# A pooled mixer computed in the other order, a three-product inverse, and a weight split placed later

## The chip, the cores and the metric

One core of one Trainium2 chip runs the whole program in one launch. The metric is the device time of the launch in microseconds, here the median of three runs of the kernel before: 2472.41 us (2469.35 to 2473.65).

## What is computed

A stack of three blocks on x of 512 tokens by 1024 features, all in f32. Block one is a gated delta rule mixer with 8 heads and a gated feed-forward. Then comes a modulated norm, a **pooled mixer** and a feed-forward with a short convolution, then differential attention and another such feed-forward, and a last norm. The parts that matter here:

```python
def modulate(h, shift, scale): return h * (1.0 + scale) + shift
# end of block one, which is the input of the pooled mixer's residual
x = modulate(rms_norm(x, normf_w), shf, scf)
# the delta rule, per head and chunk
t_inv = triangular_solve(eye + lower, eye, lower=True, unit_diagonal=True)
# pooled mixer on rms_norm(x, mix_norm)
for g, win in enumerate((2, 4, 8, 16)):       # 256 features each
    mean = (cs[hi] - cs[lo]) / (hi - lo)      # moving mean over tokens, window win, cut at the ends
    parts.append(mean - x_g)
y = einsum('bsgc,gce->bsge', pooled, w) * scale
```

## The kernel before

**Layout.** Activations lie feature-major: `x[:, m]` is 128 features by 512 tokens, eight such tiles. A product of f32 accuracy is made of three of rounded operands (`fp32r`): `term` (L1854 on) issues w_hi by h_hi, w_hi by h_lo and w_lo by h_hi, each with 512 moving columns. Every 128-column block of every weight is a "tile": SP loads it into `raw` (two slots), ScalarE copies it to `w_hi`, VectorE writes `w_lo = raw - w_hi` (L1111), and TensorE uses it. Both `split`s run four tiles ahead of TensorE and wait in their engine's queue for the slot that the product of four tiles before used. So weights stream in program order, and each engine's program places its own splits by hand among its other work.

**The heads.** `head` (L2005 for TensorE, L1334 for VectorE, L837 for ScalarE, L586 for POOL) computes one head of the delta rule while TensorE fills its waits with the next head's weight tiles. The tables HEAD_FILL and LAST_FILL say how many eighths of a tile (three products) stand ahead of each step. The inverse is built in six levels by doubling blocks. With X the inverse so far and U its transpose, a level does: `y` = masked lower part by X (bank 4), VectorE adds the identity into y_t; `u` = y_t by u_t (bank 6), ScalarE copies it to u_t; TensorE turns u_t (`x` step, bank 5), and VectorE copies that to x_t for the next level. VectorE and ScalarE also do the next head's short convolutions (`conv_taps`, `conv_silu`, `conv_tap`) and splits between these steps; the first split after the fifth level on ScalarE and the `short_conv` on VectorE need weight tile 4 of the head to be finished.

**A norm.** `norm` (L1949) sums squares over features by TensorE with one-column products (`sums`), VectorE writes mean plus eps (L1133), POOL takes the power -1/2 (L560), TensorE spreads it over rows (bank 3), and VectorE multiplies x by it. POOL adds up the first seven squares while a projection runs, ScalarE makes the last. Ahead of the mean VectorE has the last weight split of the projection behind it.

**The pooled mixer.** After the first feed-forward's down projection (DOWN[0], L1608) a norm writes the new x (`normed`), with squares for a second norm. That norm's factor is spread, and VectorE builds for each group of two feature tiles the sums over 2, 4, 8 and 16 tokens by doubling (`double`, L444; POOL does the widest), corrects the ends with `edges`, subtracts the centre (L1662), ScalarE and VectorE split the result into p_hi and p_lo, TensorE multiplies it with W in 48 wide products, and VectorE adds it to x (L1682).

**SP** loads in the order of its program. Four small loads for the attention stand behind the three ATT_Q tiles, with a wait until the down projection before is finished, and ahead of the next tiles' loads:

```python
sp.wait_ge(tile_done, ATT_Q.tile0)
for n, name in enumerate(("diff_lam_q1_2", "diff_lam_k1_2", "diff_lam_q2_2", "diff_lam_k2_2")):
    sp.dma_start(lam_in[0:1, n, :], a[name]).then_inc(lam_in_s, 16)
```

## Time and profile before

| | |
|---|---|
| median of 3 runs | 2472.41 us |
| the profiled execution, its own time | 2468.45 us |
| its span | 2466.8 us |
| TensorE busy | 2238.9 us (91%) |
| VectorE busy | 1315.5 us (53%) |
| ScalarE busy | 873.1 us (35%) |
| POOL busy | 652.0 us (26%) |
| chain that ended last | PE 72%, DVE 13%, issue 7%, ACT 4%, DMA 1%, POOL 1% |

Busy time is the time in which an engine has an instruction under way; a matmul's end is modelled, so the distance of two starts tells more than one's length. The chain is followed back from the last instruction to what released it. DVE is VectorE, ACT ScalarE, PE TensorE, SP the engine that issues loads.

### The profile page before, as it was taken

What the parts mean: (1) busy time and instruction counts of PE and PEld (TensorE: products, weight loads), DVE (VectorE), ACT (ScalarE), POOL (GpSimd) and SP (SyncE); (2) the same over time, 40 slices, a digit from 0 to 9 for tenths busy, and PEclk for the clock granted to TensorE, in tenths of its full rate; (3) what the DMA queues carried; (4) which work ended last, traced back from release to release, by engine and by line L of the source; (5) the groups of instructions that cost most, each with busy time, mean ns of one, the idle gap of its engine ahead of it and who ended that gap; (6) DMA issues with size and microseconds to landing.
All of it is one profiled execution on the core that took longest, in us unless ns stands there. A gap on an engine that the chain in (4) does not pass through costs nothing.

```text
span 2466.8 us, 31197 instructions
## 1 busy us (share of the span) xinstructions
PE 2238.9 (91%) x10502; PEld 1800.6 (73%) x10502; DVE 1315.5 (53%) x1755; ACT 873.1 (35%) x1287; POOL 652.0 (26%) x645
## 2 busy tenths in 40 slices
PE   5799999999889989999984999998888886999998
PEld 5677777777778868888873888887666564888887
DVE  6667655665643444334337544432676766444432
ACT  1322322232212223232223544421565654444421
POOL 3378666776660030000112000011032322000011
PEclk6999999999989999999996999999899997999999
DMA  6333333332323322333330233333111110333332
GB/s 213 84 100 93 85 86 101 95 87 84 95 69 95 99 79 85 97 98 90 98 94 17 85 94 95 96 94 95 46 43 60 43 60 26 94 94 101 91 94 73
DMA packets 351925, 211.44 MB, mean 86 GB/s; under 512 B 8649, under 2 KB 339843, under 8 KB 351876
## 3 DMA queue, kind: packets, MB, share of 16 engines
q1 hardware_dynamic: 343130, 184.67, 25.8%
q0 software_dynamic: 7680, 25.17, 3.4%
q10 hardware_dynamic: 1065, 0.96, 0.1%
q8 instruction: 29, 0.48, 0.1%
q14 instruction: 21, 0.16, 0.0%
HBM read 208.67 MB, written 2.10 MB: 85 GB/s over the span
## 4 chain that ended last, share of the span: by engine, by line
PE 72%; DVE 13%; issue 7%; ACT 4%; DMA 1%; POOL 1%; ACTq 0%; DVEq 0%; POOLq 0%; SPq 0%
PE ps L1858 21%; PE ps L1860 20%; PE ps L1859 20%; PE ps L2027 4%; PE ps L1896 3%; ACT at_swap L1020 2%; DVE w_lo L1111 1%; DVE small L1768 1%; ACT w_hi L697 1%; DVE gd_y_t L1422 1%; DVE gd_x_t L1445 1%; PE ps L1976 1%; DMA ada<-w_ada 1%; DVE gd_q_g L1410 1%; DVE at_rot L1746 0%
## 5 line engine op out<-in xcount | busy, mean ns | idle before, releaser
L1858 PE MATMUL ps<-h_hi,w_hi 128*128 128x512 f32 x1896 | 778.2, 410 | 28.3 <-DVE h_lo L1178 7.0
L1111 DVE TENSOR_TENSOR w_lo<-raw,w_hi 128x1024 fp32r<-128x1024 f32 x335 | 449.9, 1344 | 601.8 <-ACT w_hi L697 601.0
L1860 PE MATMUL ps<-h_hi,w_lo 128*128 128x512 f32 x1896 | 751.7, 396 | 0.0
L1859 PE MATMUL ps<-h_lo,w_hi 128*128 128x512 f32 x1896 | 750.1, 396 | 0.0
L697 ACT ACTIVATE w_hi<-raw 128x1024 fp32r<-128x1024 f32 x335 | 354.0, 1058 | 726.4 <-PE ps L1860 675.0
L1858 PEld LDWEIGHTS ps<-h_hi,w_hi 128*128 128x128 f32 x1896 | 364.1, 192 | 98.3 <-issue 25.2
L1860 PEld LDWEIGHTS ps<-h_hi,w_lo 128*128 128x128 f32 x1896 | 362.5, 191 | 79.1
L1859 PEld LDWEIGHTS ps<-h_lo,w_hi 128*128 128x128 f32 x1896 | 364.2, 192 | 65.6
L547 POOL TENSOR_TENSOR sq_sum<-x 128x512 f32<-128x512 f32 x5 | 5.2, 1040 | 947.5 <-DVE x L1620 522.3
L1858 PE MATMUL ps<-act_hi,w_hi 128*128 128x512 f32 x528 | 205.4, 389 | 0.0
L1859 PE MATMUL ps<-act_lo,w_hi 128*128 128x512 f32 x528 | 205.4, 389 | 0.0
L1860 PE MATMUL ps<-act_hi,w_lo 128*128 128x512 f32 x528 | 205.4, 389 | 0.0
L591 POOL TENSOR_TENSOR ada_w<-ada_w 128x256 f32<-128x256 f32 x144 | 132.3, 918 | 11.3
L1858 PEld LDWEIGHTS ps<-act_hi,w_hi 128*128 128x128 f32 x528 | 99.1, 188 | 20.6
L1860 PEld LDWEIGHTS ps<-act_hi,w_lo 128*128 128x128 f32 x528 | 99.1, 188 | 20.6
L1859 PEld LDWEIGHTS ps<-act_lo,w_hi 128*128 128x128 f32 x528 | 99.1, 188 | 20.6
L591 POOL TENSOR_TENSOR ada_w<-ada_w,cact 128x512 f32<-128x512 f32 x96 | 109.9, 1144 | 2.9 <-DMA ada_w<-w_ada 2.0
L674 POOL TENSOR_TENSOR x<-x,wo_s 128x512 f32<-128x512 f32 x56 | 74.2, 1342 | 112.8 <-ACT wo_s L1045 112.8
L551 POOL TENSOR_TENSOR sq_tmp<-x 128x512 f32<-128x512 f32 x31 | 34.9, 1127 | 226.3 <-DVE x L1620 144.8
L976 ACT ACTIVATE act_hi<-tmp 128x512 f32 x66 | 41.7, 632 | 131.4 <-DVE tmp L1602 87.7
L1605 DVE TENSOR_TENSOR act_lo<-tmp,act_hi 128x512 f32 x66 | 45.7, 693 | 61.1 <-ACT act_hi L976 61.1
L875 ACT ACTIVATE gd_u_t<-ps 128x512 f32<-128x512 f32 x48 | 28.6, 595 | 131.6 <-PE ps L2027 131.6
(314 smaller groups left out, 2850.1 us busy)
## 6 DMA issues: line engine op xcount, KB each, us to landing
raw<-ffn_w_up SPq DMA_DIRECT2D x88, 512.0 KB, 3.8
raw<-w_in SPq DMA_DIRECT2D x72, 512.0 KB, 3.8
raw<-w_ffn_in SPq DMA_DIRECT2D x44, 512.0 KB, 3.8
ada_w<-w_ada POOLq DMA_DIRECT2D x64, 256.0 KB, 3.3
raw<-ffn_w_down SPq DMA_DIRECT2D x32, 512.0 KB, 3.6
raw<-diff_w_qkv SPq DMA_DIRECT2D x24, 512.0 KB, 3.7
ada<-w_ada SPq DMA_DIRECT2D x4, 2048.0 KB, 15.3
ada_w<-w_ada_f POOLq DMA_DIRECT2D x32, 256.0 KB, 3.2
```

Of the source, the lines that this page charges most:

```text
L591: nc.gpsimd.tensor_tensor(dst, a, b, op).then_inc(ada_own, 1)
L674: nc.gpsimd.tensor_tensor(x[:, m], x[:, m], wo_s[:, m % 4], ADD).then_inc(wo_add, 1)
L697: nc.scalar.activation(w_hi[:, tile.slot], raw[:, tile.raw], ACT.Copy).then_inc(hi_ready, 1)
L976: nc.scalar.activation(dyn(act_hi, 2 * i + j), tmp[:, 4 + j], ACT.Copy).then_inc(f_hi, 1)
L1020: swapped = nc.scalar.activation(at["swap"][32 * q:32 * q + 32], ps[32 * (q ^ 1):32 * (q ^ 1) + 32, b, :], ACT.Copy)
L1111: nc.vector.tensor_tensor(w_lo[:, tile.slot], raw[:, tile.raw], w_hi[:, tile.slot].bitcast(F32), SUB)\
L1605: nc.vector.tensor_tensor(dyn(act_lo, 2 * i + j), gu, dyn(act_hi, 2 * i + j).bitcast(F32), SUB)\
L1858: nc.tensor.matmul(dst, w_hi[:, tile.slot, k], hi, start=first, stop=False)
L1859: nc.tensor.matmul(dst, w_hi[:, tile.slot, k], lo, start=False, stop=False)
L1860: return nc.tensor.matmul(dst, w_lo[:, tile.slot, k], hi, start=False, stop=last)
L1896: return nc.tensor.transpose(dst, src, ident[0:n_rows, 0:n_rows])
L2027: ins = nc.tensor.matmul(part(bank(b), n), part(lhs, n), part(rhs, n), start=True, stop=True)
```

## The change

Three parts.

**The inverse.** x_{n+1} is no longer u_t turned but a product of its own from the old u_t and y_t, issued ahead of the u products. The fills are quarters of a tile (six products) now, with no fill between x and u except at the last level, and none ahead of the w products.

```diff
-HEAD_FILL = dict(kv_tokens=2, g_rows=2, kk_qk=2, kb_rows=4, x_pairs=6, y0=1, w=1, o_sums=4, o_norm_rows=4)
...
+HEAD_FILL = {name: 1 for name in PE_STEPS if name != "w" and name not in [f"u{_n}" for _n in range(LEVELS - 1)]}
+HEAD_FILL.update(kb_rows=2, x_pairs=3, o_sums=2, o_norm_rows=2)
+LAST_FILL = {name: 1 for name in ["kv_tokens", "g_rows", "kk_qk", "kb_rows"] + [f"y{_n}" for _n in range(LEVELS)]}
+LAST_FILL.update(x_pairs=2, o_sums=2, o_norm_rows=2)
...
                     by_chunk(4, low_part[n % 2], x_t).then_inc(g_pe, 1)
+                    fill(f"x{n}")
+                    after_dve(f"y{n}")
+                    if n:
+                        after_act(f"u{n - 1}")
+                    if n < LEVELS - 1:
+                        by_chunk(5, u_t, y_t).then_inc(g_pe, 1)
                     fill(f"u{n}")
-
-                    after_dve(f"y{n}")
                     by_chunk(6, y_t, u_t).then_inc(g_pe, 1)
-                    if n < LEVELS - 1:
-                        fill(f"x{n}")
-                        after_act(f"u{n}")
-                        by_chunk(5, u_t, None, True).then_inc(g_pe, 1)
```

TensorE, head loop, before: from the u products of the third level (gd_u_t, gd_y_t) to the fill behind the turn of u_t (cst, gd_u_t). Products with h and w are fills.

```order
L2027 MATMUL ps<-gd_u_t,gd_y_t 128x128 [waits g_dve]
L2027 MATMUL ps<-gd_u_t,gd_y_t 128x128 x3
L1858 MATMUL ps<-h_hi,w_hi 128x512
L1859 MATMUL ps<-h_lo,w_hi 128x512
L1860 MATMUL ps<-h_hi,w_lo 128x512
L2020 REGISTER_ALU
L1896 MATMUL ps<-cst,gd_u_t 128x128 [waits g_act]
L1896 MATMUL ps<-cst,gd_u_t 128x128 x3
L1858 MATMUL ps<-h_hi,w_hi 128x512
```

The same place after the change: from the wait for y_t.

```order
L2016 REGISTER_ALU
L2019 REGISTER_ALU [waits g_dve]
L2026 MATMUL ps<-gd_y_t,gd_u_t 128x128 [waits g_act]
L2026 MATMUL ps<-gd_y_t,gd_u_t 128x128 x3
L2026 MATMUL ps<-gd_u_t,gd_y_t 128x128 x4
L1866 MATMUL ps<-h_hi,w_hi 128x512
L1867 MATMUL ps<-h_lo,w_hi 128x512
L1868 MATMUL ps<-h_hi,w_lo 128x512
```

The turn and the fill ahead of it are gone; eight products of x and u stand together (x first), and the fill behind them is twice as long.

**The late split.** `token_factor` takes the last tile of the stage before and splits it after the mean is written; the loops of the projections are written out so that their last output leaves this split out. In the same move the four small attention loads go to `masks`, which is free by then, ahead of the second feed-forward's tiles, and SP's wait is gone.

```diff
-            def token_factor(r):
+            def token_factor(r, late=None):
                 if r != N_MIX:
                     mean_squares(r)
+                if late is not None:
+
+                    split(late)
+
                 dve.wait_ge(n_pe, 2 * r + 2)
...
+            sp.wait_ge(tile_done, DOWN[0].tile(9, 1).before + 1)
+            sp.dma_start(bands[:], a["const_bands"]).then_inc(bands_in, 16)
             sp.dma_start(pos_i[0:1, :], a["positions_2"].rearrange("(o t) -> o t", o=1)).then_inc(pos_in, 16)
+            for n, name in enumerate(("diff_lam_q1_2", "diff_lam_k1_2", "diff_lam_q2_2", "diff_lam_k2_2")):
+                sp.dma_start(lam_in[:, n // 2, n % 2], a[name]).then_inc(lam_in_s, 16)
```

VectorE at the attention's norm, before: the last update of x, the split, the loop's end, the mean (small<-ps), the first use of the factor.

```order
L1620 TENSOR_TENSOR x<-x,ps 128x512
L1110 REGISTER_ALU
L1111 TENSOR_TENSOR w_lo<-raw,w_hi 128x1024 [waits hi_ready]
L1629 REGISTER_ALU
L1629 COMPARE_AND_BRANCH
L1133 TENSOR_SCALAR small<-ps 128x4 [waits n_pe]
L1187 SCALAR_TENSOR_TENSOR tmp<-x,vec,ps 128x512 [waits n_pe]
```

After the change:

```order
L1630 TENSOR_TENSOR x<-x,ps 128x512 [waits tile_done]
L1140 TENSOR_SCALAR small<-ps 128x4 [waits n_pe]
L1118 TENSOR_TENSOR w_lo<-raw,w_hi 128x1024 [waits hi_ready]
L1186 SCALAR_TENSOR_TENSOR tmp<-x,vec,ps 128x512 [waits n_pe]
```

The split now stands behind the mean, and the loop's branch is gone.

**The mixer.** W is applied first, on x as the down projection leaves it. With G = (1 + scale) * normf_w * mix_norm per feature, `weighted` makes h_hi and h_lo = split of x * G inside the down projection's loop, and sums over features of x times W_CROSS and of (scaled x) squared, from which both norms' factors come (five small linked operations, one more power on POOL). TensorE multiplies token-major: for each of four token blocks and two halves of features 12 products of 256 columns (`z_piece`), with x as the stationary operand; twelve more per half for the shift vector (`shift_products`). VectorE turns each result into z_tok = PSUM * factor + shift_z. The moving means, minus the centre, are a constant band matrix, loaded to `bands`, scaled by the second factor per token, and applied in 32 f32 products of 129 to 143 columns.

```diff
+                def weighted(m, b, before):
+
+                    dve.wait_ge(out_used[b], before + 1)
+                    if m:
+                        dve.wait_ge(pl_cross, m)
+                        nc.vector.scalar_tensor_tensor(cross, x[:, m], col(wsc[:, W_CROSS], m), cross, MULT, ADD).then_inc(pl_cross, 1)
...
+                    if m == KD - 1:
+                        mean_squares(N_OUT1)
+                    weighted_lo(m)
...
+            def z_piece(n, p):
+
+                tile = POOLW.tile(p, 0)
...
+                for g in (0, 1):
+                    for k in (0, 1):
+                        c = 4 * p + 2 * g + k
+                        dst = bank(Z_BANK[n, p])[:, 2 * P * g:2 * P * g + 2 * P]
+                        last = z_term(dst, tile, g, k, part(h_hi[:, c], n), part(h_lo[:, c], n))
...
+            sums(N_OUT1, shift_products)
+            z_piece(0, 0)
+            shift_products(1)
+            pe.wait_ge(n_pool, N_OUT1 + 1)
+            rows_of(3, S_RSTD).then_inc(n_pe, 1)
...
+            for n in (1, 2, 3):
+                z_piece(n, 0)
+            for n in range(NC):
+                z_piece(n, 1)
+
+            pe.wait_ge(bands_ready, NC)
+            for m in range(KD):
+                g = m // 2
+                b = open_out(POOLW.out(m, 0))
+                pe.wait_ge(z_ready, NC * (m // 4 + 1))
+                for n in range(NC):
+                    lo, hi = band_span(n, g)
+                    last = nc.tensor.matmul(bank(b)[:, lo:hi], part(z_tok[:, n], m), bands[:, n, g, 0:hi - lo],
+                                            start=n == 0, stop=n == NC - 1, skip_group_check=True)
```

VectorE in the mixer, before: from the position cast through the second mean and the first group's ladder (win, pool_d).

```order
L1638 CAST pos_f<-pos_i 1x512 [waits pos_in]
L1641 MEMSET win_114 128x1056
L1133 TENSOR_SCALAR small<-ps 128x4 [waits n_pe]
L1650 TENSOR_TENSOR win_l_117<-x,ps 128x2x512 [waits n_ht,pl_pool,edges_in,n_pe]
L1650 TENSOR_TENSOR win_114<-x,ps 128x2x512 [waits pl_dve]
L444 TENSOR_TENSOR win_115<-win_114 128x2x526 [waits pl_dve]
L1659 TENSOR_TENSOR win_115<-win_115,edges 128x2x2x8 [waits pl_dve]
L1662 SCALAR_TENSOR_TENSOR pool_d<-win_115,win_114 128x1024 [waits pl_dve]
```

After the change: from the last update of x in the down projection to the second of the five small operations.

```order
L1140 TENSOR_SCALAR small<-ps 128x4 [waits n_pe]
L1648 SCALAR_TENSOR_TENSOR h_lo<-x,wsc,h_hi 128x512 [waits pl_hi]
L1654 TENSOR_TENSOR tmp<-tmp 128x512 [waits pl_scaled,pl_sq]
L1118 TENSOR_TENSOR w_lo<-raw,w_hi 128x1024 [waits hi_ready]
L1666 CAST pos_f<-pos_i 1x512 [waits pos_in]
L1676 SCALAR_TENSOR_TENSOR z_tok<-ps,small,shift_z 128x512 [waits pl_z,shift_out,n_pool,n_pe]
L1683 SCALAR_TENSOR_TENSOR tmp<-x,wsc,ps 128x512 [waits pl_scaled]
L1683 SCALAR_TENSOR_TENSOR tmp<-x,wsc,ps 128x512
L1702 TENSOR_TENSOR small<-ps,small 128x4 [waits pl_sums]
L1703 TENSOR_TENSOR small<-small,ps 128x4 [waits pl_own]
L1704 TENSOR_TENSOR small<-small 128x4 [waits pl_own]
```

The second mean and the ladder are gone; what follows is z_out (z_tok), outer (tmp) and the small operations, in turn with four more of each behind them.

## Rows read from the trace of the kernel before

**Rows 1.** Windows, one head: us; busy PE, PEld, DVE, ACT, POOL; clock; DMA; GB/s.
```profile
344.00:425.00 81.00, 74.97 (x413) 59.41 (x412) 50.91 (x77) 22.67 (x43) 56.47 (x62) 0.98 0.32 91
```

**Rows 2.** Timeline of PE, mixer: start us, length us, operation [idle before].
```profile
1282.43 0.39 PE L1859 MATMUL ps<-act_lo,w_hi 128*128 128x512 f32 x1
1282.66 0.39 PE L1860 MATMUL ps<-act_hi,w_lo 128*128 128x512 f32 x1
...
1355.48 0.77 PE L1858 MATMUL ps<-h_hi,w_hi 128*128 128x512 f32 x1 [2.32 <-DVE h_lo L1178]
```

**Rows 3.** The page's first line.
```profile
span 2466.8 us, 31197 instructions
```

**Rows 4.** Timeline of PE in the fourth head, its inverse.
```profile
358.42 1.16 PE L2027 MATMUL ps<-gd_x_t,gd_low_d 128*128 128x128 f32 x8
...
376.34 1.16 PE L2027 MATMUL ps<-gd_x_t,gd_dia 128*128 128x128 f32 x8
...
379.38 1.16 PE L2027 MATMUL ps<-gd_u_t,gd_y_t 128*128 128x128 f32 x8 [0.49 <-DVE gd_y_t L1422]
...
381.23 0.66 PE L1896 MATMUL ps<-cst,gd_u_t 128*128 128x128 f32 x4
...
382.67 1.16 PE L2027 MATMUL ps<-gd_x_t,gd_low_d 128*128 128x128 f32 x8
...
394.00 1.16 PE L2027 MATMUL ps<-gd_u_t,gd_k_beg 128*128 128x128 f32 x8 [1.63 <-ACT gd_u_t L875]
```

**Rows 5.** Timelines of ACT and DVE in that head.
```profile
392.41 1.06 ACT L697 ACTIVATE w_hi<-raw 128x1024 fp32r<-128x1024 f32 x1 [4.67 <-PE ps L1860]
...
384.47 2.52 DVE L1309 SCALAR_TENSOR_TENSOR gd_v_s<-ps,vec,gd_v_s 128x511 f32<-128x511 f32 x3
...
398.81 0.28 DVE L1471 COPY gd_y_t<-ps 128x128 f32<-128x128 f32 x1
```

**Rows 6.** Timeline of PE in the last head: two levels' starts.
```profile
702.68 1.13 PE L2027 MATMUL ps<-gd_x_t,gd_low_d 128*128 128x128 f32 x8 [0.18 <-DVE gd_x_t L1445]
...
707.98 1.13 PE L2027 MATMUL ps<-gd_x_t,gd_dia 128*128 128x128 f32 x8 [0.88 <-DVE gd_x_t L1445]
```

**Rows 7.** Timelines of PE and DVE, norm after the output projection.
```profile
914.34 1.05 PE L1946 MATMUL ps<-cst,tmp 128*128 128x1 f32 x8 [0.94 <-ACT tmp L743]
...
916.41 0.15 DVE L1133 TENSOR_SCALAR small<-ps 128x4 f32<-128x4 f32 x1
```

**Rows 8.** Timeline of DVE around the mixer.
```profile
1285.71 1.23 DVE L1111 TENSOR_TENSOR w_lo<-raw,w_hi 128x1024 fp32r<-128x1024 f32 x1 [1.64 <-ACT w_hi L697]
...
1346.07 0.75 DVE L1682 SCALAR_TENSOR_TENSOR x<-ps,vec,x 128x512 f32<-128x512 f32 x1
...
1353.20 1.41 DVE L1187 SCALAR_TENSOR_TENSOR tmp<-x,vec,ps 128x512 f32<-128x512 f32 x2 [2.31 <-PE ps L1896]
```

**Rows 9.** Timelines of PE, ACT and DVE at the attention's norm.
```profile
1718.78 0.70 PE L1946 MATMUL ps<-cst,tmp 128*128 128x1 f32 x5
...
1721.90 1.06 ACT L697 ACTIVATE w_hi<-raw 128x1024 fp32r<-128x1024 f32 x1 [3.53 <-DMA raw<-diff_w_qkv]
...
1724.13 0.15 DVE L1133 TENSOR_SCALAR small<-ps 128x4 f32<-128x4 f32 x1
```

**Rows 10.** Timeline of PE in the fourth head: products of one column.
```profile
415.46 1.48 PE L2094 MATMUL ps<-cst,ada_s 128*128 128x1 f32 x12
```

**Rows 11.** Windows, the prologue's loads (columns as in group 1).
```profile
20.00:42.00 22.00, 15.27 (x72) 15.29 (x72) 18.08 (x16) 2.08 (x2) 13.10 (x10) 0.54 0.93 321
```

**Rows 12.** DMA issues: tile, queue, count, KB each, median us to landing.
```profile
raw<-ffn_w_up SPq DMA_DIRECT2D x88, 512.0 KB, 3.8
```

**Rows 13.** Timeline of PE in the fourth head, at its second level of clock.
```profile
420.34 0.63 PE L1859 MATMUL ps<-h_lo,w_hi 128*128 128x512 f32 x1
420.76 0.63 PE L1860 MATMUL ps<-h_hi,w_lo 128*128 128x512 f32 x1
```

**Rows 14.** Tile gd_k_s, the turns: ns min/median/max, first and last start.
```profile
L1896 PE MATMUL ps<-cst,gd_k_s x32: 271/273/332, 103.0 to 664.3; 128*128 128x128 f32 x32
```

More of the change, by code:

```diff
@@ L999, in _ @@
                 square(N_FFN0, m)
-            for t in range(2):
-                split(POOLW.tile(t, 0).ahead())
+            split(POOLW.tile(1, 0).ahead())
             normed_hi(N_FFN0)
@@ L1717, in _ @@
+            split(POOLW.tile(0, 0).ahead())
+            for m in range(KD):
+                b, before = POOLW.out(m, 0)
+                dve.wait_ge(pl_out, m + 1)
+                dve.wait_ge(n_ht, scaled_base(N_OUT1) + m + 1)
+                nc.vector.scalar_tensor_tensor(x[:, m], bank(b), vec[:, V_PSC + m:V_PSC + m + 1], x[:, m], MULT, ADD)\
+                  .then_inc(out_used[b], 1)
+                if m >= 3:
+                    add_square(N_FFN0, m - 2)
             add_square(N_FFN0, KD - 2)
-            for t in range(2):
-                split(POOLW.tile(t, 0).ahead())
```

401 lines of the change are left out of this document (204 added, 197 removed).

## The prediction

> **What bounds the kernel now.** I read four views. First the windows of busy time, by stage: in a stretch that holds one head of the gated delta rule (81 us) TensorE is busy 75 us at a granted clock of 0.98 [rows 1], so the heads are close to bound by TensorE, and a saving there must come out of its own work or its short waits. Then TensorE's timeline of one head, for these waits. Then the timelines of all engines between the last product of the first down projection and the first product of the next up projection. There TensorE has 48 wide products and some small ones to do in 72.4 us (1283.05 to 1355.48) [rows 2]: that stretch is bound by VectorE, which does two norms, a ladder of shifted sums and the splits. Last the places where a norm's mean is taken, for what stands ahead of it in VectorE's queue. The profiled execution took 2468.45 us, its span is 2466.8 [rows 3], and it lies 4.0 us under the median of the runs, 2472.41; I take the sum from the first and put the same difference on the median.
>
> **The inverse in the heads.** A level starts with the y products and now runs y, VectorE's y_t, u products, ScalarE's u_t, turn of u_t, VectorE's x_t, next y: four changes of engine on one chain, covered by four eighths of a weight tile. In the level of [rows 4] it is 376.34 to 382.67, 6.33 us; six levels and the step to the w products take 358.42 to 394.00, 35.6 us [rows 4]. After the change x comes straight from u_t and y_t by a product, beside u's, so the chain is y, y_t, x, x_t, next y, and u_t leaves it. TensorE's work per level: four f32 products (eight records) take from 379.38 to the next fill at about 0.91 us; the turn about 0.41; a fill of three products 0.68 plus about 0.1 for each change of form. Before: 0.91 + 1.46 + 0.91 + 0.79 + 0.41 + 0.79 = 5.27, the rest of the 5.6 to 6.3 being waits. After: y 0.91, a quarter (six products, 1.46), x and u together 1.72, a quarter 1.46, that is 5.55 with no wait if VectorE keeps up: y_t needs at most 3.0 us from the start of y (376.34 to 379.38, with VectorE late) and 2.4 of them are covered; x_t has 3.2 us from the start of x and needs about 2. So per level about 0.3 us more work and about 0.6 us less waiting. At the last level tile 4 now ends before the u products and not after them. ScalarE's split that needs it stood ahead of the last u_t: it waited 4.67 us and started at 392.41 [rows 5], so u_t and w were held to 394.00. That gives some 1.3 us of the gain. VectorE's short convolution needs the same tile and ended so late that the first state copy ran at 398.81 [rows 5]; it moves up by the same amount, so the gain is not lost there. Walking the stretch with these prices: the first fill is one eighth longer (+0.5), five levels at 5.55 to 5.6, the last 4.5, together 33.0 instead of 35.6: **2.6 us for each of seven heads, 18.2**. In the last head a level takes 5.3 us (702.68 to 707.98) [rows 6], bound by the hops; without the turn 5.1, but a quarter fills where an eighth did; four eighths move to the two late fills, partly in the open: 2.3 us. Heads together **20.5**. Lower bound: VectorE's taps (2.5 us [rows 5]) now stand between y_t and a much earlier x at two levels; where u and the quarter behind x cover only 1.4 of them, 1.1 is lost each time, which leaves 0.4 a head. Upper: TensorE's remaining waits shrink too, 3.3 a head (my estimate, by half of what I leave in the stretch).
>
> **Late weight split.** Ahead of a norm VectorE splits one more weight tile before it writes the mean squares. In the norm after the output projection the sums end at 914.34 + 1.05 = 915.39 and the small operation runs at 916.41 [rows 7]: 0.96 us is the split; the same pair stands at the mixer's first norm (inside the term below). The split (1.23 [rows 8]) then lies under POOL's power and TensorE's rows, and its tile isn't needed before the fourth product. At the feed-forward norm behind the attention the split is not on the path: 0. At the attention's own norm more hangs on it: sums end at 1718.78 + 0.70 = 1719.48, but SP holds the load of the tile behind a wait for the end of the down projection and four small loads; ScalarE waited 3.53 us for the data, to 1721.90, VectorE split after it, and the mean came at 1724.13 [rows 9]. The change moves the four loads far ahead and drops the wait, so the mean comes at 1719.6: **4.5**. With the first, **5.5**.
>
> **The mixer.** Removed: the second norm of the mixer (squares, sums, power, rows), the ladder, the memsets, the split of the pooled input on the path. Added in the down projection: two vector products and one sum per output on VectorE, two activations on ScalarE, about 2.1 and 1.4 us in a period of 15 us in which both mostly wait; nothing, except for the last output. Added behind it: on TensorE 24 + 96 products of 256 columns and 32 f32 band products of about 135; on VectorE 8 copies out of PSUM with shift, 8 outer products, 5 tiny linked operations, 2 scalings of bands.
>
> No row shows a product of 256 columns with rounded operands. Bounds: a pair of weight load and one-column product takes 0.12 us (twelve in 1.48) [rows 10]; a 512-column one 0.23 (1282.43 to 1282.66) [rows 2]. I take 0.12, nearest to the first, since half the columns should stream in half of 0.23 us while the next load runs; 0.23 stays for the range. The band products, four-pass f32, take 0.23 each by the y products (0.91 for four), 0.9 per output.
>
> The Trainium skill (TensorE: Matmul & The Clock Gate, section LDWEIGHTS) says that a weight load costs by its columns alone, 128/1.2 = 107 ns, however narrow the product is, which speaks against cutting products in half. By it the 120 pairs would cost at least 12.8 us, against 14.4 by my price; the row of one-column pairs, 0.12 us each, agrees.
>
> TensorE from the end of the down projection: sums 0.9, to 1284.0; shift products 1.4; last sums after the last square, 1286.2; first piece of W 1.4; shift products 1.4; rows 0.4, to 1289.6; nine small products (18 records) 2.0; seven pieces 10.1, to 1301.8. VectorE: x, cross, mean (1286.3), last low part, last scaled sum, split, cast, to 1289.4, then it waits for rows to 1289.7. From there it is the one that bounds: 8 + 8 operations at 0.66 (two in 1.41 [rows 8]) 10.6; five links at 0.25, 1.3; two scalings 1.2, to 1302.8; then the split of one tile, which waits for ScalarE behind its last shift, to 1305.4. POOL's second power lies under outer products. Band products have begun by then, so the eight updates run at VectorE's pace: x(7) starts at about 1313.2 where it started at 1346.07 [rows 8]. From x(7) to the next product nothing changes (9.4 us), so 1355.48 becomes 1322.6: **32.9**. Lower bound 22 (pairs at 0.23, below); upper 35 (tiny links free, no late split).
>
> On SP the load of the bands (1.18 MB) and five small loads now stand ahead of the next weight loads, behind a wait for the third-last tile of the down projection (42 products at 0.227 before 1283.05, so about 1273.5). At 321 GB/s, the best stretch [rows 11], it takes 3.7 us, the next tile 1.6 more; a tile alone lands after 3.8 [rows 12], so some 2 us are latency, and the next tile lands near 1281, where it was wanted at 1279; ScalarE and VectorE reach the last x at 1283.3 just in time. I cost it at 0; if loads run slower it costs up to 4.
>
> **Sum.** 20.5 + 5.5 + 32.9 = 58.9. 2468.45 - 58.9 = 2409.6 for the profiled run, 2472.4 - 58.9 = **2413.5** on the median, taken as 2413.
>
> **Rivals.**
>
> A. Loads and narrow products do not overlap: 0.23 a pair. For: in every wide product 0.23 hides one load, so no row shows a load hidden in 0.11. Against: f32 pairs of 128 columns go at 0.11. TensorE's chain then ends at 1314 instead of 1302 and the updates start 10 us later: 2423. Chance 0.12.
>
> B. VectorE's queue in the heads. It is in order, and taps, splits and gates stand between y_t and the copy x_t, whose input now comes about 1.3 us after y_t (x's four products and the hops). For: VectorE already held y_t back by up to 0.6 us at some levels. Against: u and a quarter lie behind x. At the lower bound of 0.4 a head 15.4 us are lost on seven heads: 2429. Chance 0.16.
>
> C. The bands' load comes late, or ScalarE behind it: the last square and with it the mixer start 4 us later: 2417. Chance 0.1, in the range anyway.
>
> D. Slower. In the heads TensorE's short waits move, and with 0.3 us pauses next to one longer one behind the last u products the granted clock falls from 0.98 to its lower level, 1.2 GHz, where a product takes 0.42 us (420.34 to 420.76) instead of 0.23 [rows 2, 13]. It decides at +58.9 us: 7.4 us a head, 37 of 192 products at the low level, a clock under about 0.85 in the heads. Against: one such piece of eight products per head is all the trace shows, behind the w products' stretch, and pauses get shorter. Chance 0.03.
>
> The Trainium skill (TensorE: Matmul & The Clock Gate, section A second HAM failure mode: psum-queue depth-cycling) tells of clocks that fall by many micro-pauses between groups; the 0.98 of [rows 1], with a pause at nearly each level, disagrees for this kernel.
>
> E. The change doesn't do what it says: the late mean could still be held, since in the mixer VectorE's queue also waits for ScalarE's low-part inputs. It would leave 5.5 of the sum out: 2419. Chance 0.02.
>
> **How the numbers follow.** The forecast has 0.57, A 0.12, B 0.16, C 0.10, E 0.02, D 0.03. The forecast's own bounds: heads 0.5 us either way on eight heads (4), mixer 2 up and 5 down, so 2404 to 2421. The range takes in A, B and C: 2404 to 2432; A and B together (2439) and D stay out. A measurement of this kernel can tell 0.2%, some 5 us. Every case but D is faster by far more: faster 0.97, and D's 0.03 is split into same 0.01 and slower 0.02.
>
> **What would show it.** The distance from head to head, (664.3 - 103.0)/7 = 80.2 us by the first turn of k [rows 14], falls to about 77.6, with no turn of u_t but the first; ScalarE's split ahead of the last u_t no longer waits 4.7 us. Mean squares follow their sums within 0.2 us, the attention's too. From the last down product to the next up product about 39.5 us, VectorE nearly without idle between 1290 and 1303 on the old clock, 256-column products at 0.12. The prediction is wrong if the heads keep 80 us, or if TensorE's pieces take over 2 us each.

## The result, and the profile after

The changed kernel takes **2433.34 us** (median of 4 runs, 2430.36 to 2437.41) where the kernel before takes 2472.97 (4 runs, 2469.35 to 2473.65): ratio 0.9844, 95% interval 0.9827 to 0.9861, or 39.6 us less. Forecast were 58.9 less and 2413, with a range up to 2432. The direction was right; the time lies outside the range, a third of the gain is missing. The profiled execution took 2435.78 us. The page of the changed kernel: its first line, the busy times, and the chain that ended last by engine.

```profile
span 2434.1 us, 31707 instructions
...
PE 2255.2 (93%) x10796; PEld 1845.2 (76%) x10796; DVE 1309.9 (54%) x1766; ACT 873.6 (36%) x1291; POOL 641.5 (26%) x640
...
PE 73%; DVE 14%; issue 7%; ACT 4%; DMA 1%; POOL 1%; ACTq 0%; DVEq 0%; POOLq 0%; SPq 0%
```

TensorE's busy time has **grown**, 2238.9 to 2255.2. Part of it is work: 294 more products (10796 for 10502), and the mixer keeps TensorE busy 34.6 us instead of 29.3. But 10.6 of the 16.3 us stand in the three down projections, whose products are the same 1584; that is the first sign that something in its long streams is slower.

The span cut at the same events in both profiled executions (starts of the first and last turn of k [rows 14], of the first row product behind it, of the first and last products of the gates and of each down projection, of the first product behind each norm). Differences of times of the trace, in us:

| stretch | before | after | difference | forecast |
|---|---|---|---|---|
| to the first turn of k | 103.0 | 104.6 | +1.6 | 0 |
| seven heads | 561.0 | 545.5 | -15.5 | -18.2 |
| last head, to the gates | 111.8 | 115.3 | +3.5 | -2.3 |
| gates | 87.7 | 88.6 | +0.8 | 0 |
| output projection and norm | 57.8 | 57.6 | -0.2 | -1.0 |
| three up projections and their norms, attention | 1085.1 | 1085.5 | +0.4 | 0 |
| three down projections | 358.4 | 368.9 | **+10.6** | 0 |
| mixer | 72.8 | 42.9 | -30.0 | -32.9 |
| attention's norm | 12.4 | 8.6 | -3.8 | -4.5 |

(The last stretches add up with 16.7 at the end to 2466.8 and 2434.1; the forecast's difference is put on the same cuts.) The first row is no effect of the change: over the kernels below, with either inverse and either mixer, the first turn starts anywhere from 103.2 to 106.0. The mixer and the looped heads came nearly as walked. What is missing is mostly in three down projections, whose instructions on TensorE the change doesn't touch, and in the last head.

**Down projection.** TensorE's timeline of the changed kernel, the first and the last of the 528 products of the first one; then the first of before, whose last is in [rows 2].

```profile
1153.53 0.40 PE L1866 MATMUL ps<-act_hi,w_hi 128*128 128x512 f32 x1
...
1276.50 0.40 PE L1868 MATMUL ps<-act_hi,w_lo 128*128 128x512 f32 x1
```

```profile
1163.21 0.39 PE L1858 MATMUL ps<-act_hi,w_hi 128*128 128x512 f32 x1
```

122.97 us where it was 119.45 (1163.21 to 1282.66): 233.3 ns from product to product and 226.7 before, at a granted clock of 1.00 in both. All three do the same.

**Inverse.** TensorE's timeline of the fourth head, which answers to [rows 4]; then ScalarE's, to [rows 5].

```profile
355.20 1.05 PE L2026 MATMUL ps<-gd_x_t,gd_low_d 128*128 128x128 f32 x8
...
367.34 1.05 PE L2026 MATMUL ps<-gd_x_t,gd_low_d 128*128 128x128 f32 x8
...
372.78 1.05 PE L2026 MATMUL ps<-gd_x_t,gd_dia 128*128 128x128 f32 x8
...
375.05 1.05 PE L2026 MATMUL ps<-gd_y_t,gd_u_t 128*128 128x128 f32 x8
375.94 1.06 PE L2026 MATMUL ps<-gd_u_t,gd_y_t 128*128 128x128 f32 x8
...
378.22 1.05 PE L2026 MATMUL ps<-gd_x_t,gd_low_d 128*128 128x128 f32 x8
...
389.35 1.16 PE L2026 MATMUL ps<-gd_u_t,gd_k_beg 128*128 128x128 f32 x8 [0.74 <-ACT gd_u_t L874]
```

```profile
387.75 1.06 ACT L694 ACTIVATE w_hi<-raw 128x1024 fp32r<-128x1024 f32 x1 [4.16 <-PE ps L1868]
```

From y to y the last three of the five levels take 5.44 us (372.78 to 378.22 is one), where I walked 5.55 and it was 5.6 to 6.3; the first two take 5.8 and 6.4; x and u stand together without a wait. The stretch is 34.15 us instead of 35.6. The wait of ScalarE's split didn't go: 4.16 us where it was 4.67, but the u_t behind it now holds w by 0.74 only.

**Mixer.** TensorE's timeline, which answers to [rows 2]; then VectorE's, to [rows 8].

```profile
1285.33 0.28 PE L2165 MATMUL ps<-w_hi,h_lo 128*128 128x256 f32 x1
1285.45 0.28 PE L2166 MATMUL ps<-w_lo,h_hi 128*128 128x256 f32 x1
...
1295.29 1.95 PE L2209 MATMUL ps<-bands,z_tok 128*128 128x129 f32 x16
1299.13 8.29 PE L2209 MATMUL ps<-bands,z_tok 128*128 128x130 f32 x48 [1.90 <-DVE x L1725]
...
1319.37 0.77 PE L1866 MATMUL ps<-h_hi,w_hi 128*128 128x512 f32 x1 [2.32 <-DVE h_lo L1177]
```

```profile
1283.39 0.75 DVE L1676 SCALAR_TENSOR_TENSOR z_tok<-ps,small,shift_z 128x512 f32<-128x512 f32 x1 [0.37 <-PE ps L1893]
...
1297.19 1.22 DVE L1118 TENSOR_TENSOR w_lo<-raw,w_hi 128x1024 fp32r<-128x1024 f32 x1 [0.95 <-ACT w_hi L694]
...
1307.93 0.74 DVE L1725 SCALAR_TENSOR_TENSOR x<-ps,vec,x 128x512 f32<-128x512 f32 x1
```

Put on the time axis of before (6.15 us later), VectorE's first z_out starts at 1289.5 where I had 1289.7, and x(7) at 1314.1 where I had 1313.2. The 256-column products stand 0.12 us apart (1285.33 to 1285.45), as taken. From x(7) to the next up product it is 11.4 us, and I had said that nothing changes from 9.4.

**Norm.** The norm after the output projection, by PE, DVE and POOL; its pair of before is in [rows 7], with POOL's power in the second fence.

```profile
904.52 1.05 PE L1945 MATMUL ps<-cst,tmp 128*128 128x1 f32 x8 [0.72 <-ACT tmp L742]
907.84 1.11 PE L1893 MATMUL ps<-cst,small 128*128 128x128 f32 x4 [2.26 <-POOL small L564]
...
905.61 0.16 DVE L1140 TENSOR_SCALAR small<-ps 128x4 f32<-128x4 f32 x1 [1.81 <-PE ps L1945]
905.69 1.22 DVE L1118 TENSOR_TENSOR w_lo<-raw,w_hi 128x1024 fp32r<-128x1024 f32 x1
...
905.85 1.93 POOL L564 TENSOR_TENSOR small<-small 128x4 f32<-128x4 f32 x1 [4.15 <-DVE small L1140]
```

```profile
916.64 1.02 POOL L560 TENSOR_TENSOR small<-small 128x4 f32<-128x4 f32 x1 [5.11 <-DVE small L1133]
```

The mean follows its sums at once, as forecast. But POOL's power, which runs beside VectorE's split now, takes 1.93 us and not 1.02. What the late split gives (0.96) the power takes back (0.91).

### The profile page after: what moved, and what is told of

It is laid out like the page before. It is cut to its first block, busy times and chain, and to the rows that moved or that the text cites. A ratio compares the mean times of both kernels' runs of the same rounds, so it can differ in the third digit from the quotient of the medians.

```text
span 2434.1 us, 31707 instructions
## 1 busy us (share of the span) xinstructions
PE 2255.2 (93%) x10796; PEld 1845.2 (76%) x10796; DVE 1309.9 (54%) x1766; ACT 873.6 (36%) x1291; POOL 641.5 (26%) x640
## 3 DMA queue, kind: packets, MB, share of 16 engines
q1 hardware_dynamic: 343130, 185.82, 26.2%
## 4 chain that ended last, share of the span: by engine, by line
PE 73%; DVE 14%; issue 7%; ACT 4%; DMA 1%; POOL 1%; ACTq 0%; DVEq 0%; POOLq 0%; SPq 0%
PE ps L1866 21%; PE ps L1868 21%; PE ps L1867 21%; PE ps L2026 3%; PE ps L1893 2%; ACT at_swap L1027 2%; DVE w_lo L1118 1%; DVE small L1777 1%; DVE small L1447 1%; DVE gd_y_t L1421 1%; DVE gd_q_s L1308 1%; ACT w_hi L694 1%; DVE gd_q_g L1409 1%; PE ps L1975 1%; DMA ada<-w_ada 1%
## 5 line engine op out<-in xcount | busy, mean ns | idle before, releaser
L1118 DVE TENSOR_TENSOR w_lo<-raw,w_hi 128x1024 fp32r<-128x1024 f32 x335 | 439.1, 1312 | 587.2 <-ACT w_hi L694 586.1
L1866 PEld LDWEIGHTS ps<-h_hi,w_hi 128*128 128x128 f32 x1896 | 364.5, 192 | 114.2 <-issue 37.7
L595 POOL TENSOR_TENSOR ada_w<-ada_w 128x256 f32<-128x256 f32 x144 | 123.7, 859 | 11.3
L671 POOL TENSOR_TENSOR x<-x,wo_s 128x512 f32<-128x512 f32 x56 | 74.3, 1343 | 112.8 <-ACT wo_s L1052 112.8
```

The source lines that it names most:

```text
L595: nc.gpsimd.tensor_tensor(dst, a, b, op).then_inc(ada_own, 1)
L671: nc.gpsimd.tensor_tensor(x[:, m], x[:, m], wo_s[:, m % 4], ADD).then_inc(wo_add, 1)
L1118: nc.vector.tensor_tensor(w_lo[:, tile.slot], raw[:, tile.raw], w_hi[:, tile.slot].bitcast(F32), SUB)\
L1866: nc.tensor.matmul(dst, w_hi[:, tile.slot, k], hi, start=first, stop=False)
```

## The experiments

Eleven kernels ran, each beside the kernel before on its chip. Names that begin with a_ are the changed kernel with an alteration, those with b_ the kernel before with one. Since a profile shows one execution and the runs of one kernel spread by up to 19 us (why, is a result below), verdicts rest on stretches of the traces, with the medians beside them.

### Where the tiles start: a_pad and b_shift

All tiles of one partition are laid end to end. The change alters the small ones ahead of the wide ones: scales, small values and edges took 640 bytes, scales, the shift's two parts and small values take 608. So everything behind them starts 32 bytes earlier, and is no longer at a multiple of 64.

```diff
-        small = sb("small", [P, 80])
+        small = sb("small", [P, 88])
```

> The changed kernel with one number altered: the tile of small values is 8 columns wider, so that every tile allocated behind it, the activations of the down projections among them, starts 32 bytes later. In the changed kernel the sum of the tiles ahead of them is 32 bytes off a multiple of 64, before it was a multiple of 64. Theory (place): the wide products of the three down projections stand 233.3 ns apart after the change and 226.7 before, only because of where their moving operand starts; 1584 products by 6.67 ns are 10.6 us, 96 of the gate's another 0.6 to 1.3. The kernel should take about 2421.5 and the distance in the down projections go back to 226.7. Rival (work): the distance comes from other work of the change beside the down projections (the longer program of VectorE, the loads). Then it stays at 233.3 and the time at 2433.

> The kernel before, with the tile of small values 8 columns wider and nothing else: now its activations start 32 bytes off a multiple of 64. Theory (place): down projections at 233.3 ns a product, 11 to 12 us more, about 2484. Rival (work): no difference, 2472 to 2473. If the heads read their tiles more slowly from there too, the distance from head to head (80.1 us) grows and the sum is over 12.

Measured: a_pad 2426.22 us (2422.59 to 2430.01), ratio to before 0.9815 (0.9798 to 0.9832); b_shift 2486.44 (2481.11 to 2487.85) beside 2471.26, ratio 1.0064 (1.0048 to 1.0081). TensorE's timelines of the same 528 products, of a_pad and of b_shift:

```profile
1157.55 0.39 PE L1866 MATMUL ps<-act_hi,w_hi 128*128 128x512 f32 x1
...
1277.00 0.39 PE L1868 MATMUL ps<-act_hi,w_lo 128*128 128x512 f32 x1
```

```profile
1165.98 0.40 PE L1858 MATMUL ps<-act_hi,w_hi 128*128 128x512 f32 x1
...
1288.95 0.40 PE L1860 MATMUL ps<-act_hi,w_lo 128*128 128x512 f32 x1
```

119.45 us in a_pad, 122.97 in b_shift: the second number of each kernel, exchanged by 32 bytes. The gates, half of whose products read such a tile, are 87.7 and 88.5. That is 11.4 us for three down projections and the gates. The theory of the place stands, the rival falls. By the medians the pad gives 7.1 us in the changed kernel and costs 15.2 in the other one; on top of the 11.4 lies what single executions differ by (seven heads 549.1 in a_pad's profile and 545.5 in the changed kernel's, for one). The other guess in the text of b_shift does not hold: seven heads take 561.1 us there and 561.0 before, so products of 128 columns on tiles in the same place pay nothing that shows.

The Trainium skill (SBUF — State Buffer, section Operand start alignment) has a rule for where an operand may start, a multiple of its element size, and says that it is about legality and not speed; what a start costs in time is told by these runs alone.

### The split beside the power: a_early and a_mid

Both have the wider tile too, so their neighbour is a_pad. a_early puts the split ahead of the mean again; a_mid behind the fifth scaled tile. These are lines of a_mid's edit; its second half stands in both kinds of norm.

```diff
-                if late is not None:
-
-                    split(late)
-
                 dve.wait_ge(n_pe, 2 * r + 2)
...
                     if m:
                         lo(m - 1)
+                    if m == 4 and late is not None:
+                        split(late)
```

> The changed kernel with the wider small tile, and the weight split put back ahead of the mean squares in the four norms that take it late; the small loads stay where the change has them. Theory (shared): a split of VectorE that runs beside POOL's power stretches it, 1.02 us before and 1.93 after the change, so that the late split gives 0.96 and takes back 0.91. Ahead of the mean it costs about 1 us at the norm after the output projection and at the attention's norm and frees 0.9 at all four, so about 1.8 us less than the same kernel with the late split, 2419.5 to 2420, and POOL's power is 1.02 again. Rival (as predicted): the late split is worth 1 us a norm, and this run is 2 to 4 us slower than its neighbour with the late split.

> The changed kernel with the wider small tile, and the late weight split moved once more: VectorE does it after the fifth scaled tile of the norm, when POOL has long finished the power and TensorE already multiplies. Theory (shared): POOL's power takes 1.02 us again and the mean still follows its sums at once, so each of four norms gets 0.9 us back: 3.6 us less than its neighbour with the late split, 2422.6 against 2426.2, if VectorE is ahead of TensorE by then. Rival: the split delays the last low parts of the norm and TensorE waits for them, or for the split tile itself, and the 0.9 is lost again: 2426.

Measured: a_early 2420.18 (2410.90 to 2426.24), a_mid 2417.51 (2407.05 to 2425.59), against 2426.22. In a_mid, DVE and POOL at the same norm:

```profile
903.87 0.16 DVE L1140 TENSOR_SCALAR small<-ps 128x4 f32<-128x4 f32 x1 [2.01 <-PE ps L1947]
...
912.57 1.22 DVE L1118 TENSOR_TENSOR w_lo<-raw,w_hi 128x1024 fp32r<-128x1024 f32 x1
...
904.11 1.02 POOL L564 TENSOR_TENSOR small<-small 128x4 f32<-128x4 f32 x1 [4.34 <-DVE small L1140]
```

POOL's power is 1.01 or 1.02 us at the last six norms of both, 1.92 or 1.93 at four norms of a_pad. The attention's norm takes 8.57 us in a_pad, 8.64 in a_early and 7.41 in a_mid: early and late are worth the same, and only the split in the middle gains, 1.2 here and 0.7 in the two kernels at the end. So the 3.8 us that the change won there come from the loads moved ahead, and not from the split. The mixer takes 42.9 in a_pad and 39.5 and 39.8 in these two; of those 3.3 us the power explains 0.9 and the rest is TensorE's clock: the 24 last band products run in 6.63 us in a_early, in 8.29 in the changed kernel, and the sums behind them are faster too. The band products stand ahead of the split that these two kernels move, and they take 6.63 in a_last below as well, which leaves it alone: that the clock held there is luck of the execution, not the split's doing. Such luck is in the two medians too; what the place of the split is worth is the 0.9 at each of four norms.

The Trainium skill (SBUF — State Buffer, section Who interferes with whom) says that a VectorE instruction with two inputs in SBUF contends with a GpSimd instruction that reads SBUF, and the one that comes second waits for all of the first. The split has two such inputs; POOL's power began 0.16 us behind it (905.69, 905.85) and ended 0.87 us behind its end, where it takes 1.02 alone; the trace agrees, nearly all of the split was waited for. It shows the wait as busy time.

### The last head and the clock: b_inv, a_last, a_ada, b_ada

b_inv is the kernel before with the new inverse and its fills alone. a_last moves two late quarters of the last head up:

```diff
-LAST_FILL.update(x_pairs=2, o_sums=2, o_norm_rows=2)
+LAST_FILL.update(x_pairs=2, x0=1, x2=1, o_sums=1, o_norm_rows=1)
```

> The kernel before with the inverse of three products and its quarter fills, nothing else of the change. Theory (late fills): the seven looped heads give 2.2 us each, 15.5, and the last head gives nothing but loses 4, because its fills ahead of the last sums and rows hold 24 wide products where there were 12, and they run at the lower clock (0.42 us each): together about 11.5, so 2461. Rival (as predicted): 20.5 us, 2452, if the loss of the last head in the changed kernel came from elsewhere.

> The changed kernel with the wider small tile; in the last head two of the four late quarters (ahead of the sums and ahead of the rows) move up to stand before the x products of the first and the third level, where TensorE waits 1.5 and 2.5 us. Theory (late fills): the last head took 69.2 us after the change and 65.3 before, because 12 more wide products stood at its end, at 0.42 us each; it should fall by 4 to 5 us, to about 64.5, and the kernel to 2421.5. Rival (inverse): the last head is longer for its shorter cover between the levels; then nothing is gained by the move, or less than 1 us.

Measured: b_inv 2455.29 (2447.49 to 2462.91), ratio 0.9926 (0.9902 to 0.9950), with seven heads at 549.1 and the last at 69.2, as in a_pad (549.1, 69.2): the loss of the last head shows with the inverse part alone. But part of it is not the program's: b_shift, whose heads are those of the kernel before, has its last head at 67.5 where the kernel before had 65.3. The profiled execution of b_inv is the slowest of its runs, near the 2461 of the theory; the median lies between the two expectations. a_last 2425.47 (2421.89 to 2427.02), no gain: the last head falls to 67.4, not to 64.5. Another kernel, a_mix below, which leaves the heads alone, had its last head at **65.0**. The ends of the two last heads, TensorE's last long wait, its sums and its row product behind the late quarters, of the changed kernel and of a_mix:

```profile
704.36 0.49 PE L2081 MATMUL ps<-gd_q_g,state 128*128 128x128 f32 x2 [1.81 <-DVE gd_y_t L1470]
...
705.82 0.77 PE L2076 MATMUL ps<-state,gd_x_t 128*128 128x128 f32 x2 [0.29 <-DVE state L1476]
...
712.71 0.95 PE L2090 MATMUL ps<-cst,gd_dec 128*128 128x1 f32 x8
...
719.28 0.60 PE L1893 MATMUL ps<-cst,small 128*128 128x128 f32 x4
```

```profile
706.56 0.49 PE L2083 MATMUL ps<-gd_q_g,state 128*128 128x128 f32 x2 [1.04 <-DVE gd_y_t L1471]
...
712.18 0.95 PE L2092 MATMUL ps<-cst,gd_dec 128*128 128x1 f32 x8
...
717.20 0.60 PE L1895 MATMUL ps<-cst,small 128*128 128x128 f32 x4
```

Twenty products of one column and twelve wide ones stand between; they take 6.57 us in the one and 5.02 in the other. In a_mix no wide product of that end stands 0.42 or 0.43 us behind the one before it, in the changed kernel 16 do, in the kernel before 5. So what the last head costs is mainly the clock at its end; where two quarters stand is worth at most 1.8.

The clock falls twice in the changed kernel's last head: first from 705.82 on, ahead of the narrow products and behind a wait of 1.81 us for VectorE, and again behind them. The two traces whose last head is 65.0 (a_mix, and a_best2 below) waited 1.04 and 1.00 at that place, and all eight others with the new inverse waited 1.80 to 1.86 and took 67.4 to 69.3. VectorE's instruction ahead of that y_t is a weight split, which takes 2.24 us in the changed kernel and 1.47 in a_mix, beside POOL's products for the modulation. No run tests this wait, and the kernel before fell there too with a wait of 1.10, so the cause of the first fall stays open.

The looped heads show the same. Turns of k of the changed kernel, one per head:

```profile
417.98 0.66 PE L1893 MATMUL ps<-cst,gd_k_s 128*128 128x128 f32 x4 [1.05 <-DVE og_lo L1502]
496.37 0.66 PE L1893 MATMUL ps<-cst,gd_k_s 128*128 128x128 f32 x4 [1.05 <-DVE og_lo L1502]
573.16 0.66 PE L1893 MATMUL ps<-cst,gd_k_s 128*128 128x128 f32 x4 [1.05 <-DVE og_lo L1502]
650.01 0.63 PE L1893 MATMUL ps<-cst,gd_k_s 128*128 128x128 f32 x4 [1.14 <-DVE og_lo L1502]
```

78.4 us, then 76.8 twice. The windows of two of these heads (columns as in group 1):

```profile
418.00:496.30 78.30, 74.31 (x430) 63.35 (x430) 50.60 (x76) 22.18 (x43) 56.65 (x62) 0.98 0.33 93
496.40:573.10 76.70, 72.68 (x430) 62.15 (x430) 50.64 (x76) 22.17 (x43) 56.35 (x62) 1.00 0.33 94
```

Granted clock 0.98 and 1.00. The 1.6 us are some seven products at the low level, 0.43 us apart (490.36 to 490.79 and on), and this is what TensorE did before:

```profile
486.73 0.95 PE L2090 MATMUL ps<-cst,gd_dec 128*128 128x1 f32 x8
487.54 1.48 PE L2093 MATMUL ps<-cst,ada_s 128*128 128x1 f32 x12
488.88 0.48 PE L1866 MATMUL ps<-h_hi,w_hi 128*128 128x512 f32 x1
...
490.36 0.63 PE L1866 MATMUL ps<-h_hi,w_hi 128*128 128x512 f32 x1
490.79 0.63 PE L1867 MATMUL ps<-h_lo,w_hi 128*128 128x512 f32 x1
```

Twenty products of one column, then six wide ones, and the clock is at 1.2 GHz. a_ada and b_ada break this run in two: the twelve for the modulation come a quarter of a tile ahead of the eight sums.

```diff
-                fill("o_sums")
-
-                after_dve("o_sum")
...
+                fill("ada")
+                pe.wait_ge(g_pool, step(POOL_STEPS, "ada", h))
+                for j in range(6):
+                    nc.tensor.matmul(bank(5)[:, 8 + j:9 + j], ada_s[:, j], one_col, start=True, stop=True)
+                fill("o_sums")
+
+                after_dve("o_sum")
```

> The changed kernel with the wider small tile; in every head the 12 products of one column for the modulation stand one quarter of a tile ahead of the 8 one-column sums, instead of right behind them. Theory (narrow run): the granted clock falls to its lower level about 1.5 us behind the run of 20 one-column products, in most heads, and costs 1.6 us each time (76.8 us from head to head where it doesn't, 78.4 where it does). With the run broken in two it falls less often: seven heads 538 to 542 us instead of 549, the kernel 2415 to 2420. Rival (waits): the clock falls for the 1.1 us wait ahead of the next head or for something else; the distance stays at 78.4, the time at 2426, or is a little over it since the wait for POOL comes earlier.

> The kernel before, with the 12 one-column products of the modulation two eighths of a tile ahead of the 8 sums in the looped heads, nothing else. In the kernel before three of seven heads took 80.9 to 81.7 us and four 79.3 to 79.4. Theory (narrow run): all seven at 79.3 or less, 555 us instead of 561, the kernel 5 to 6 us less, 2465. Rival: the lower clock has another cause in the kernel before, 2471.

Measured: a_ada 2414.98 (2410.06 to 2417.48), 11.2 less than a_pad, as expected; b_ada 2466.96 (10 runs, 2464.72 to 2470.33) beside 2473.39, ratio 0.9977 (0.9967 to 0.9986). The first and the last turn of k in a_ada:

```profile
103.21 0.60 PE L1893 MATMUL ps<-cst,gd_k_s 128*128 128x128 f32 x4
...
640.64 0.63 PE L1893 MATMUL ps<-cst,gd_k_s 128*128 128x128 f32 x4 [1.14 <-DVE og_lo L1502]
```

Seven heads in 537.4 us, every one at 76.7 to 76.9. In b_ada six are at 79.3 and one at 80.2, 556.0 instead of 561.0. The two kernels at the end, which have the same edit, don't fall in any of their 14 looped heads. In all, the distance shows the fall in 51 of the 63 looped heads where the 20 stand together (6 of 14 with the old inverse, 45 of 49 with the new one) and in 1 of the 28 where they stand apart. So in the looped heads the run of narrow products sets off most of the falls, in both kernels; it doesn't do so each time. With the old inverse the count is small, but the medians of 10 and 14 runs, 6.4 us apart, go with it. And the inverse is worth 79.3 - 76.8 = **2.5 us a head**: I had 2.6.

It also explains the spread. Seven heads with 1.6 us each and a last head of 65.0 or 69.2 make 15.4 us; the runs of b_inv lie 15.4 apart (those of a_mid 18.5, a little more). That the spread comes from there is an inference, since only one execution of each is in a trace.

The Trainium skill (TensorE: Matmul & The Clock Gate, section A second HAM failure mode: psum-queue depth-cycling) tells of a kernel whose clock falls for short pauses between groups of products. In these heads pauses don't sort the cases: the changed kernel pauses less than before (TensorE is busy 74.3 of 78.3 us of a head, 75.0 of 81 in [rows 1]) and fell in more heads (five of seven are at 78.4, in a_pad all seven; before, three at 80.9 to 81.7), and a_ada, which moves only the narrow products and what must wait for them, doesn't fall. For the looped heads the measurement decides for the narrow products.

### The mixer's queue: a_mix

```diff
-            split(POOLW.tile(0, 0).ahead())
             for m in range(KD):
+                if m == 3:
+                    split(POOLW.tile(0, 0).ahead())
```

ScalarE also gets one wait more, ahead of its squares, until the last of x's eight tiles with the shift is written (`act.wait_ge(n_ht, scaled_base(N_OUT1) + KD)`).

> The changed kernel with the wider small tile; in the mixer VectorE's split of the next weight tile, which waits 0.95 us for ScalarE and takes 1.22 just ahead of the first update of x, stands behind the third update. Theory (queue): the first band products' banks come free 2.2 us earlier, TensorE's wait of 1.9 us behind the second output goes and with it the lower clock in the later band products; from the last down product to the next up product 40 to 41 us instead of 42.9, the kernel 2 to 3 us less, 2424. Rival: the updates run at VectorE's pace anyway and the split costs the same wherever it stands: 42.9, 2426.

Measured: 2419.82 us (2418.79 to 2426.45), the mixer 38.6 us. TensorE's timeline of the band products, which had stopped for 1.90 us at 1299.13 in the changed kernel:

```profile
1288.89 5.08 PE L2211 MATMUL ps<-bands,z_tok 128*128 128x129 f32 x40
1294.59 3.73 PE L2211 MATMUL ps<-bands,z_tok 128*128 128x132 f32 x24 [0.62 <-DVE x L1727]
...
1308.65 0.77 PE L1868 MATMUL ps<-h_hi,w_hi 128*128 128x512 f32 x1 [2.32 <-DVE h_lo L1178]
```

Twenty band products (two records each) run before the first wait now, eight did, and the wait is 0.62. The gain is 4.3 us for a split of 1.22 and its wait of 0.95: all band products take 9.4 us from first to last and not 12.1 (2.7), and from the first sum to the mean it is 1.98 and not 3.61 us (1.6), because the clock no longer falls there. How much of it is the queue's own, the traces in which the clock held in the band products without this edit (a_early, a_mid, a_last) tell: there they take 10.47 us, so 1.0 of the 2.7 is the shorter queue and 1.7 the clock. With the edit the sums to the mean take 1.98 or 1.99 in three traces of three, without it 2.77 to 3.61 in six of six: that a shorter stop keeps the clock up is likely by this count, and not shown apart from the luck of executions. The rival, which had no gain at all, falls.

### Together: a_best1 and a_best2

> The changed kernel with five alterations together: the wider small tile, the modulation's products a quarter ahead of the sums, the late split behind the fifth scaled tile, the mixer's split behind its third update, and in the last head two late quarters ahead of the x products (its one-column products stay together there). If the terms add: 2426.2 less 11.2 (ada), 3 to 5 (mixer), 3 (mean), 0 to 2 (last head) is 2406 to 2409. If the separate gains were partly the same fallen clock counted twice, 2410 to 2415.

> As its neighbour with all five, but the last head keeps its fills as the change has them, with one quarter between the modulation's products and the sums. Theory (late fills): 1 to 2 us slower than its neighbour, 2408 to 2411. Rival (inverse): equal or faster, since what costs in the last head is the lower clock behind its end and not where two quarters stand.

The first holds all the alterations so far. The second has the last head's late quarters as in a_ada, one of them ahead of the modulation's products. Measured: a_best1 2411.59 (2407.28 to 2413.26), ratio 0.9752 (0.9739 to 0.9765); a_best2 **2410.07** (2407.00 to 2410.22), ratio 0.9746 (0.9732 to 0.9759) to the kernel before: faster than both kernels (the change has 0.9844), some 23 us under the change. The first line of its page:

```profile
span 2407.4 us, 31708 instructions
```

Its stretches: seven heads 537.7, last head 65.0, gates 87.7, each down projection 119.45, mixer 37.7. The single gains don't add up: 11.2, 6.4 and 8.7 less than a_pad would give 2400. The same recovered clock was counted twice in them (in the mixer of both a_mid and a_mix). Against the theory of late fills, the neighbour that keeps them is not slower: in a_best1 the last head took 67.9, and the clock was low from the wait of 1.86 us on. The text of a_best1 says that its one-column products stay together in the last head; they don't, six wide products stand between the 12 and the 8 there (701.95 and 707.24). And a_ada, whose last head has the order of a_best2, took 67.5: one execution of each doesn't settle what that order is worth in the last head.

## Why the prediction was right or wrong

- **What bounds the kernel**: right. The heads were TensorE's, the mixer VectorE's, and both gave nearly what was read off there.
- **The inverse in seven heads**: right in size, 2.5 us a head at the same clock for 2.6. The way was in part another: in the fourth head the stretch I walked gave 1.4 us (34.15 for 35.6, two early levels at 5.8 and 6.4), the part ahead of it took 0.5, and 1.65 came behind w, where I had seen nothing: two waits of TensorE for VectorE's y_t, 0.99 and 0.49 us, are gone there. ScalarE's 4.67 us did not go. That 2.5 came so near to 2.6 is therefore in part luck. In the profiled run 15.5 instead of 18.2, since more heads ran into the lower clock.
- **The last head**: wrong. The step was "four eighths move to the two late fills, partly in the open: 2.3 us". The old table counts eighths and the new one quarters, so o_sums=2 and o_norm_rows=2 in both are 12 products before and 24 after; and the clock was low there before already. The levels did what was said: from its turn of k to the w products the last head takes 46.81 us and not 47.76. Behind w it takes 22.46 instead of 17.55, most of the difference at the lower clock (17.40 in a_mix, where the clock holds). +3.5 instead of -2.3 in the profiled run, -0.8 where the clock holds, against a kernel before in which it didn't quite.
- **Late weight split**: the mechanism was half right. Means follow their sums, and the loads moved ahead gave 3.8 us at the attention. The step that failed is "the split then lies under POOL's power": it stretches that power by 0.91 us, at four norms. The term of 5.5 came out as 4.0, and two norms that I had at 0 lost 0.9.
- **The mixer**: 30.0 for 32.9. Loads under narrow products (0.12), the five linked operations, the end of the queue at x(7): right, within 1 us. The step "from x(7) to the next product nothing changes" missed 2.0: 0.9 for the power, the rest for sums at the lower clock. Rival A is excluded by the 0.12 us.
- **Bands' load (rival C)**: priced at 0 and right. ScalarE waited 6.14 us for the tile behind it, until 1274.40 (its row stands below the list); VectorE split that tile at 1275.49 and had the last x at 1276.93, right behind TensorE's last product.
- **What I had not on the list**: the 11.4 us for tiles that start 32 bytes elsewhere. The sum had no term for it: I treated a change of small tiles as free, without a reason. It is the largest single miss, over half of the 19.8 us between 2413.5 and 2433.3, and a_pad, which undoes it, lies inside the range at 2426.22. In the profiled run the misses are 11.4 (place), 8.5 (lower clock and fills: seven heads 2.7, last head 5.8), 2.7 (power), 2.0 (rest of the mixer) and 1.6 ahead of the first turn, where executions differ by as much, 26.2 together.
- **Rivals B and D**: B's place was wrong, VectorE's queue cost the heads little (5.44 at three levels, 6.36 at one). D named the right lever, the granted clock, with the wrong trigger and a far too high bar: it never had to make the kernel slower to matter. It should have widened the range by its share.

ScalarE's timeline of the changed kernel, the split behind the bands' load:

```profile
1274.40 1.06 ACT L694 ACTIVATE w_hi<-raw 128x1024 fp32r<-128x1024 f32 x1 [6.14 <-DMA raw<-ffn_w_up]
```

## What to carry to other kernels

When a change alters the size of any tile, compute where all the tiles behind it start, and keep the rows that feed the long streams of products at a multiple of 64 bytes (the runs compare that with 32 bytes off it, nothing else); a stream whose instructions didn't change and whose pace did (count over time, to a tenth of a per cent) is the sign. Don't put VectorE work with two inputs beside a small POOL operation on the critical path: put it where TensorE is already fed. And before counting a saving of some us in a stage where the granted clock falls now and then, list what TensorE does ahead of each fall in the trace, since one such place per loop can be worth more than half of the saving (1.6 us a head here, beside the 2.5 of the inverse). One execution's trace doesn't tell luck from effect there; compare the same stretch in all of them.

## What the runs showed of the hardware

- A product of 512 columns of rounded operands takes 226.7 ns with its moving rows at a multiple of 64 bytes, 233.3 with them 32 bytes off; the weights' place was the same. For products of 128 columns in the heads no difference showed (561.0 and 561.1 us).
- A product of 256 columns of rounded operands, with its load, takes 0.12 us: the load hides.
- POOL's power on 4 columns takes 1.02 us alone and 1.92 or 1.93 beside a split of 1.22 us; it is shown as busy.
- After 20 products of one column in a row the granted clock fell to 1.2 GHz in 51 of 63 looped heads of nine traces and cost about 1.6 us each time; with 12 and 8 apart it did in 1 of 28 (a_ada, b_ada and both kernels at the end).
